# Query and key projections of the second attention as seven half-size products per 1024 columns

## The chip, the core and the metric
The kernel runs on one core of one Trainium2 chip. The core has five engines with queues of their own: TensorE (PE; PEld is its weight load), VectorE (DVE), ScalarE (ACT), GpSimd (POOL), and SyncE (SP), which here only issues transfers. Each engine takes its instructions in order and waits on semaphores for the others. The metric is device microseconds of one execution, lower is better.

## What is computed
Two transformer-like blocks run one after the other on a sequence of 1024 tokens of width 1024, all in fp32. Of the second block this matters:

```python
h = rms_norm(x, norm1_g)
proj = jnp.einsum('bsd,de->bse', h, w_in)          # 1024 x 1024 by 1024 x 6144
q, k, v, bg, cg, xc = jnp.split(proj, [1024, 2048, 3072, 4096, 5120], axis=-1)
# 16 heads of 64 columns: q and k are normalised per head, then chunked attention
q = rms_norm(q.reshape(..., 16, 64), q_norm_g)
k = rms_norm(k.reshape(..., 16, 64), k_norm_g)
```

The columns of q, k and v are wanted token-major (tokens on the partitions). The other columns (bg, cg, xc) and the gates are computed feature-major inside the attention phase, as filler work for TensorE.

## The kernel before
**Arithmetic.** Each fp32 operand is split into a high part, rounded to the matmul type fp32r, and a low part, the rest. A product is three matmul passes: high by high, high by low, low by high (`three_passes`, L199). A matmul multiplies a 128x128 block of one side by 128x512 of the other into one of the 8 banks of `ps`. The high part of the activations lies in `a_hi`, the low part in `a_lo`, each 128 partitions x 8 blocks of 128 features x 1024 tokens.

**Weights.** SP loads a chunk of 1 MB into `w_raw`; GpSimd makes `w_hi` and `w_lo` of it (`pieces`, L156: four adds of zero, then four subtractions). There are two slots of each. A chunk of the "wide" kind is 512 input features x 512 columns.

**Order of the phases around the change.** `phase_norm` (L1478) does the first block's output projection, adds the residual, normalises with the next block's gain, turns the rows (transposes into `ps`), splits them into `a_hi` (ScalarE) and `a_lo` (VectorE, function `low`), and then already computes the first 512 value columns (`next_half`). `phase_tm` (L520) computes the other five groups of 512 columns: q and k (four groups, per-head normalised by VectorE after the product) and, last, the second half of v (not normalised). `phase_attention` (L1787) loads head by head from the DRAM tensor `qkv2`. At the start of it TensorE computes four products of the feature-major filler (`EARLY = 4`, 24 matmuls each, numbered x = 0 to 3); after x = 1 and x = 2 it turns the first head's queries and keys (`round_`), and then the scores begin. `phase_turn` (L211) stands at the start of each phase: every engine but TensorE waits there until the other three have arrived, which closes the buffers of the old phase.

One group of 512 columns in `phase_tm` is 8 token tiles x 8 feature blocks x 3 passes = 192 matmuls. It is done in two halves (first 512 features for all 8 tiles, then the other 512). VectorE copies each finished bank to `stage_tm`, squares, reduces, scales; ScalarE takes the root and issues the 2 MB store of the group.

**Engine load in the MLP, for comparison.** The last phase, `phase_mlp` (L2553), already multiplies by Strassen's scheme. Its instructions there serve as rows for the new ones here: ScalarE's `w_hi` (L2892), GpSimd's `w_lo` (L2795), VectorE's `a_lo` (L3019), its additions of a bank to `res` (L3099) and its sums of two quarters (L3014).

Of the kernel before, what the change touches and what calls it, by code (L numbers as in the profile page):

```python
# [13 lines left out]
P = 128  # L14
T = 1024
# [29 lines left out]
class Tally:  # L45


    def __init__(self, sem):
        self.sem, self.base = sem, 0
# [5 lines left out]
def program(nc, io, out):  # L55
    ctx = ExitStack()
    with ctx:
# [17 lines left out]
        ext2 = dram("ext2", (16, P, 768))  # L75
        row1 = dram("bias_row1", (8, 512))
# [26 lines left out]
        W_V2 = seg(io["w_in_2"], 0, 2048, 2, wide=2)  # L103
        W_QK2 = seg(io["w_in_2"], 0, 0, 8, wide=2)
        seg(io["w_in_2"], 0, 2560, 2, wide=2)
# [378 lines left out]
        mm_tm = sem("mm_tm")  # L484
        ev_tm = sem("ev_tm")
        st_tm = [sem(f"st_tm{s}") for s in range(2)]
        tm_chunks = [2]
        tm_stores = [0, 0]
# [17 lines left out]

        def wide_first(pe, n, slot, c):

            pe.wait_ge(split_done, n + 1)
            for t in range(NT):  # L510
                pe.wait_ge(ev_tm, c * 8 + (2 * t - 6))
                wide_unit(t, t, slot, 0).then_inc(mm_tm, 1)

        def wide_second(pe, n, slot):

            pe.wait_ge(split_done, n + 1)
            for t in range(NT):
                wide_unit(t, t, slot, 1).then_inc(mm_tm, 1)

        def phase_tm(start, sections, dst, stored):  # L520

            per, width = 2, 512
            groups = sum(n for n, _, _ in sections)
            count = groups * per
            c0 = tm_chunks[0]
            tm_chunks[0] += count
            v0 = list(tm_stores)
            tm_stores[0] += (groups + 1) // 2  # L530
            tm_stores[1] += groups // 2
            heads = width // HD
            with ExitStack() as mem:
                phase_turn()
                stage = sb(mem, f"stage_tm{start}", [P, 2, NT, width])
                if any(normed for _, _, normed in sections):
                    square = sb(mem, "head_square", [P, NT * heads, HD])
                    hst = sb(mem, "head_stat", [P, 6, NT * heads])
                    h_sq, h_root, h_self, h_done = sem("h_sq"), sem("h_root"), sem("h_self"), sem("h_done")
                feed(block, start, count, lambda j: (mm_tm, j * 8 + (c0 * 8 + 8)))  # L540
                dst_v = dst.rearrange("(t p) n -> p t n", p=P)
                unstored = []

                def each_chunk(eng, body):

                    j0 = 0
                    for n, col0, normed in sections:
                        if n > 1:
                            with eng.Fori(0, n // 2) as i:
                                for q in range(2):  # L550
                                    body(i * 2 + (j0 + q), q, i + j0 // 2, i * (2 * width) + (col0 + q * width), normed)
                        if n % 2:
                            body(j0 + n - 1, 0, (j0 + n) // 2, col0 + (n - 1) * width, normed)
                        j0 += n

                @block.tensor
                def _(pe):
                    def chunk(j, q, before, col, normed):
                        wide_first(pe, j * 2 + start, slot_of(start), j * 2 + c0)
                        wide_second(pe, j * 2 + (start + 1), slot_of(start + 1))  # L560
                    each_chunk(pe, chunk)
# [60 lines left out]
        def phase_first():  # L622
# [611 lines left out]
            for r in row_in:  # L1234
                r.base += 32
# [1974 lines left out]
```

## Time and profile before
| what | value |
|---|---|
| median of 3 runs | 2184.09 us (2184.08 to 2185.55) |
| span of the profiled execution | 2181.7 us |
| median less that span | 2.4 us |
| PE busy, share of the span | 99% |
| DVE, ACT, POOL busy | 64%, 40%, 46% |
| granted TensorE clock, mean | 0.999 |

The profile shows one execution, from its first to its last instruction. What lies around the span (2.4 us) belongs to the launch. The median of the runs is what a time of the kernel means below. "Busy" of TensorE counts an instruction until its modelled end; since matmuls overlap, the spacing of their starts is what shows the pace.

### The profile page before, as it was taken

What the parts mean: (1) busy time and instruction counts of PE and PEld (TensorE: products, weight loads), DVE (VectorE), ACT (ScalarE), POOL (GpSimd) and SP (SyncE); (2) the same over time, 40 slices, a digit from 0 to 9 for tenths busy, and PEclk for the clock granted to TensorE, in tenths of its full rate; (3) what the DMA queues carried; (4) which work ended last, traced back from release to release, by engine and by line L of the source; (5) the groups of instructions that cost most, each with busy time, mean ns of one, the idle gap of its engine ahead of it and who ended that gap; (6) DMA issues with size and microseconds to landing.
All of it is one profiled execution on the core that took longest, in us unless ns stands there. A gap on an engine that the chain in (4) does not pass through costs nothing.

```text
span 2181.7 us, 29189 instructions
## 1 busy us (share of the span) xinstructions
PE 2165.9 (99%) x10570; PEld 1810.3 (83%) x10570; DVE 1406.0 (64%) x2453; ACT 862.3 (40%) x1584; POOL 994.3 (46%) x715
## 2 busy tenths in 40 slices
PE   8999999999999999999999999999999999999999
PEld 8888888888888888888888888888878888788887
DVE  7776775234445666666666493342786777898886
ACT  5555424200005555555555231212555455433332
POOL 3233465554443231313222274447465655666564
PEclk9999999999999999999999999999999999999999
DMA  6320123213225332324232473215134545826433
GB/s 230 104 75 21 45 102 140 107 43 131 96 90 154 93 93 87 106 69 112 75 99 69 167 256 118 99 62 183 59 125 157 172 145 183 327 90 229 149 123 115
DMA packets 195688, 267.17 MB, mean 122 GB/s; under 512 B 57912, under 2 KB 114008, under 8 KB 195584
## 3 DMA queue, kind: packets, MB, share of 16 engines
q1 hardware_dynamic: 119456, 189.85, 25.4%
q10 hardware_dynamic: 76128, 75.93, 11.1%
q8 instruction: 66, 1.08, 0.2%
q14 instruction: 38, 0.31, 0.0%
HBM read 190.19 MB, written 83.95 MB: 126 GB/s over the span
## 4 chain that ended last, share of the span: by engine, by line
PE 92%; DVE 3%; ACT 2%; issue 1%; POOL 1%; DMA 0%; ACTq 0%; DVEq 0%; POOLq 0%
PE ps L204 80%; PE ps L1916 3%; PE ps L1903 2%; PE ps L1891 2%; PE ps L891 1%; PE ps L866 1%; PE ps L877 1%; DVE k_lo L2137 1%; POOL w_lo L2775 1%; PE ps L1928 1%; DVE pt_lo L2185 0%; ACT pt_hi L2071 0%; PE ps L801 0%; DVE prob L2166 0%; PE ps L2410 0%
## 5 line engine op out<-in xcount | busy, mean ns | idle before, releaser
L159 POOL TENSOR_TENSOR w_hi<-w_raw,zero 128x512 fp32r<-128x512 f32 x216 | 260.3, 1236 | 865.1 <-PE ps L204 756.5
L204 PE MATMUL ps<-a_hi,w_hi 128*128 128x512 f32 x1408 | 542.9, 406 | 0.4 <-DVE q_st L1138 0.4
L204 PE MATMUL ps<-a_hi,w_lo 128*128 128x512 f32 x1408 | 523.3, 392 | 0.0
L204 PE MATMUL ps<-a_lo,w_hi 128*128 128x512 f32 x1408 | 520.6, 390 | 0.0
L204 PE MATMUL ps<-w_hi,a_hi 128*128 128x512 f32 (+1 forms) x1088 | 419.0, 385 | 3.7 <-POOL w_lo L787 2.2
L204 PE MATMUL ps<-w_hi,a_lo 128*128 128x512 f32 (+1 forms) x1088 | 417.4, 384 | 0.0
L204 PE MATMUL ps<-w_lo,a_hi 128*128 128x512 f32 (+1 forms) x1088 | 417.1, 383 | 0.0
L204 PEld LDWEIGHTS ps<-a_hi,w_lo 128*128 128x128 f32 x1408 | 264.2, 188 | 58.7
L204 PEld LDWEIGHTS ps<-a_lo,w_hi 128*128 128x128 f32 x1408 | 265.4, 189 | 41.9
L204 PEld LDWEIGHTS ps<-a_hi,w_hi 128*128 128x128 f32 x1408 | 264.8, 188 | 42.5 <-issue 0.8
L164 POOL TENSOR_TENSOR w_lo<-w_raw,w_hi 128x512 fp32r<-128x512 f32 x216 | 293.9, 1392 | 4.2
L204 PEld LDWEIGHTS ps<-w_hi,a_hi 128*128 128x128 f32 x1088 | 204.9, 188 | 45.8 <-POOL w_lo L787 2.4
L204 PEld LDWEIGHTS ps<-w_hi,a_lo 128*128 128x128 f32 x1088 | 205.0, 188 | 40.3
L204 PEld LDWEIGHTS ps<-w_lo,a_hi 128*128 128x128 f32 x1088 | 205.1, 188 | 39.9
L2185 DVE TENSOR_TENSOR pt_lo<-ps,pt_hi 128x512 fp32r<-128x512 f32 (+1 forms) x192 | 88.2, 487 | 146.7 <-ACT pt_hi L2071 146.7
L2055 ACT ACTIVATE prob<-prob,st 128x640 f32<-128x640 f32 (+4 forms) x128 | 89.4, 698 | 223.4 <-DVE st L2166 222.4
L2775 POOL TENSOR_TENSOR w_lo<-mlp_raw_b,w_hi 128x512 fp32r<-128x512 f32 x60 | 97.5, 1651 | 63.0 <-ACT w_hi L2861 63.0
L571 DVE COPY stage_tm<-ps 128x512 f32<-128x512 f32 x40 | 27.7, 691 | 149.9 <-PE ps L204 149.9
L2795 POOL TENSOR_TENSOR w_lo<-mlp_raw_more,w_hi 128x512 fp32r<-128x512 f32 x56 | 90.1, 1639 | 61.1 <-ACT w_hi L2892 61.1
L3019 DVE TENSOR_TENSOR a_lo<-mlp_part,a_hi 128x512 fp32r<-128x512 f32 x104 | 108.4, 1090 | 4.8 <-ACT a_hi L2901 4.8
L2166 DVE CUSTOM_DVE_ANT_0 prob<-ps,bias 128x640 f32<-128x640 f32 (+4 forms) x128 | 83.6, 653 | 23.5 <-issue 22.8
L2775 POOL TENSOR_TENSOR w_lo<-w_raw,w_hi 128x512 fp32r<-128x512 f32 x44 | 69.8, 1612 | 51.2 <-ACT w_hi L2861 51.2
(270 smaller groups left out, 3481.6 us busy)
## 6 DMA issues: line engine op xcount, KB each, us to landing
w_raw<-in_w_in_dram SPq DMA_DIRECT2D x32, 1024.0 KB, 5.1
mlp_part<-u_parts SPq DMA_DIRECT2D x26, 1024.0 KB, 7.8
feat_fm<-stage ACTq DMA_DIRECT2D x68, 256.0 KB, 2.0
u_parts<-mlp_acc SPq DMA_DIRECT2D x28, 512.0 KB, 2.8
u_parts<-res SPq DMA_DIRECT2D x28, 512.0 KB, 2.8
conv_in<-feat_fm ACTq DMA_DIRECT2D x24, 512.0 KB, 5.6
qkv_tm<-stage_tm ACTq DMA_DIRECT2D x5, 2048.0 KB, 6.9
res<-in_x_dram SPq DMA_DIRECT2D x16, 512.0 KB, 6.3
```

The source lines that it names most:

```text
L159: hi = nc.gpsimd.tensor_tensor(w_hi[slot][:, k:k + 2, :], w_raw[:, k:k + 2, :], zero[:, 0:1].unsqueeze(2).to_broadcast([P, 2, CW]), ALU.add)
L164: lo = nc.gpsimd.tensor_tensor(w_lo[slot][:, k:k + 2, :], w_raw[:, k:k + 2, :], w_hi[slot][:, k:k + 2, :].bitcast(F32), ALU.subtract)
L204: last = nc.tensor.matmul(out_of(o), lhs, rhs(o), start=first and n == 0, stop=final and n == 2)
L1891: last = nc.tensor.matmul(ps[:, S_BANK + bank, 0:c1 - c0], q_st[:, head_slot, b * P:(b + 1) * P], kk[:, head_slot, k0 * P + c0:k0 * P + c1 ...
L1903: last = nc.tensor.transpose(ps[:, PT_BANK + j // 4, (j % 4) * P:(j % 4 + 1) * P], prob[:, m % 4, j * P:(j + 1) * P], ident[:, :])
L1916: last = nc.tensor.matmul(ps[:, O_BANK, 0:256], v_st[:, h, kb, :], pt[:, sl, :], start=(kb == first and pt is pt_hi), stop=(kb == last_kb ...
L2055: nc.scalar.activation(prob[:, s, 0:w], prob[:, s, 0:w], ACT.Exp, scale=-1.0, bias=st[:, s, 1:2], accum_out=st[:, s, 2:3]).then_inc(exped, 1)
L2166: nc.vector.tensor_tensor_reduce(out=tile_view(prob, s, 0, nk), in0=score_view(nk), in1=tile_view(bias, hh, off, nk), scale=-1.0, scalar=3 ...
L2185: ins = nc.vector.tensor_tensor(pt_lo[:, sl:sl + cnt, cols], ps[:, bank, 0:cnt * P].rearrange("p (j n) -> p j n", n=P), pt_hi[:, sl:sl + c ...
L2775: ins = nc.gpsimd.tensor_tensor(low[:, k:k + 2, :], up_raw(p)[:, k:k + 2, :], high[:, k:k + 2, :].bitcast(F32), ALU.subtract)
L2795: ins = nc.gpsimd.tensor_tensor(down_slot(w_lo, s)[:, k, :], raw_of[p][h][:, k, :], down_slot(w_hi, s)[:, k, :].bitcast(F32), ALU.subtract)
L3019: nc.vector.tensor_tensor(down_operand(a_lo, s)[:, k, :], staged(s)[:, k, :], down_operand(a_hi, s)[:, k, :].bitcast(F32), ALU.subtract).t ...
```

## The change
Queries and keys are now computed, 1024 columns at a time (a "unit": unit 0 is q, unit 1 is k), by one step of Strassen's scheme. Tokens, features and columns are each cut in two. Seven products of 512 tokens x 512 features x 512 columns take the place of eight. The seven are called m1 to m7 and run in the order m5, m2, m4, m3, m1, m7, m6, numbered s = 0 to 13 over both units. Five of the seven need a sum of two weight quarters, five need a sum of two activation quarters. The results are added into the four quarters of the output, which lies in `res`. Each product has 4 token tiles x 4 feature blocks x 3 passes = 48 matmuls.

What moves with it:
- The second half of the value columns comes first, and ScalarE evicts and stores it. Queries and keys come last before the attention.
- ScalarE makes the weights' high part (two instructions of 128x1024 per product), GpSimd only the low part (four of 128x512). The high part of product s + 2 waits until product s has left its slot.
- VectorE sums weights, adds banks into `res`, and does the head norm per quarter (four quarters per unit). ScalarE does the squares and evicts the first two products of a unit.
- In `phase_norm` VectorE also writes an fp32 copy of the turned rows into `res` (eight copies of 128x1024 out of `ps`), which the sums need. Half of it is stored to DRAM (`spare_x`) and loaded back at the end, because two quarters of `a_hi` and `a_lo` are overwritten and the attention's filler needs them plain again (`plain_hi`, `plain_lo`).
- `ready_first` for the first head of the attention now names the stores of the quarters that hold its columns; the last store of a 2 MB value group in the attention phase goes.

The core of the diff:

```diff
-            last_store = phase_tm(W_QK2, [(4, 0, True), (1, 2560, False)], qkv2, stored2)
+            banks_read, ready_first, ready_rest = phase_qkv(stored2, spare_stored)
@@ phase_norm, vector
                     def low(t):
                         dve.wait_ge(n_hi.sem, hi0 + t + 1)
+                        if post:
+                            dve.wait_ge(*x1_stored[t % 4].at(16 * (t // 4 + 1)))
+                            nc.vector.tensor_copy(res[:, t, :].rearrange("p (k n) -> p k n", n=P), both(t))
                         nc.vector.tensor_tensor(a_lo[:, :, t * P:(t + 1) * P], both(t), ...)
@@ phase_norm, scalar
+                    def store_spare(t):
+                        act.wait_ge(n_lo.sem, lo0 + t + 1)
+                        act.dma_start(spare_x[t // 4, :, :, t % 4 * P:(t % 4 + 1) * P], turned_row(t, 0 if t // 4 else 4)
+                                      ).then_inc(spare_stored.sem, 16)
@@ new: phase_qkv
+            ORDER = ("m5", "m2", "m4", "m3", "m1", "m7", "m6")
+            COPIED = {"m5": ((0, 0, -1.0), (1, 0, 1.0)), "m2": ((0, 1, 1.0), (1, 1, -1.0))}
+            ADDED = {"m4": ((0, 0), (0, 1)), "m3": ((1, 0), (1, 1)), "m1": ((0, 0), (1, 1)), "m7": ((0, 0),), "m6": ((1, 1),)}
+            WHOLE = {"m4": (0, 1), "m3": (1, 0), "m7": (0, 0), "m6": (1, 1)}
+            SUMMED = ("m5", "m2", "m1", "m7", "m6")
+                def _(pool):
+                    for s in range(NS):
+                        for half in range(2):
+                            pool.wait_ge(*high_w.at(2 * s + half + 1))
+                            for k in (2 * half, 2 * half + 1):
+                                ins = nc.gpsimd.tensor_tensor(wide(w_lo, s)[:, k, :], raw_of[ORDER[s % 7]][:, k, :],
+                                                              wide(w_hi, s)[:, k, :].bitcast(F32), ALU.subtract)
+                        ins.then_inc(low_w.sem, 1)
+                def _(pe):
+                    for s in range(NS):
+                        p = ORDER[s % 7]
+                        pe.wait_ge(*low_w.at(s + 1))
+                        for t in range(4):
+                            (waits until copied or added of product s - 2, tile t)
+                            for k in range(4):
+                                last = three_passes(...)
+                            last.then_inc(mm_q.sem, 1)
+                    pe.wait_ge(plain_lo, 2)
+                def _(act):
+                    for s in range(NS):
+                        p = ORDER[s % 7]
+                        if p in COPIED:
+                            if s >= 7:
+                                for r, c, _ in COPIED[p]:
+                                    act.wait_ge(*store_q[r, c].at(16))
+                            for t in range(3):
+                                copy_tile(s, t)
+                        if s + 2 < NS:
+                            weight_high(s + 2)   # waits: product s done, weight sum of s + 2 done
+                        if p in COPIED:
+                            copy_tile(s, 3)
+                        if p in WHOLE:
+                            squares(s)           # one ACTIVATE of 128x2048, then the root
+                        if s == NS - 2:
+                            for n, q in enumerate(("m4", "m3")):
+                                act.wait_ge(*spare_in.at(16 * (n + 1)))
+                                nc.scalar.activation(operand(q)[0], (rd, rb)[n], ACT.Copy).then_inc(plain_hi, 1)
+                def _(dve):
+                    for s in range(NS):
+                        p = ORDER[s % 7]
+                        if p in ADDED:
+                            for t in range(4):
+                                add_tile(s, t)   # one 128x512 addition per quarter named in ADDED
+                        ahead = {1: 3, 2: 3, 3: 3, 5: 2, 6: 2}.get(s % 7)
+                        if ahead is not None and s + ahead < NS:
+                            weight_sum(s + ahead)   # two of 128x1024
+                        if p in WHOLE:
+                            norm_heads(s)        # reduce, six small ones, four products of 128x512
+                        if s == NS - 2:
+                            for n, q in enumerate(("m4", "m3")):
+                                dve.wait_ge(plain_hi, n + 1)
+                                nc.vector.tensor_tensor(operand(q)[1], (rd, rb)[n], ...).then_inc(plain_lo, 1)
```

## Rows read from the trace of the kernel before

**Rows 1.** The page: busy time and share of each engine
```profile
PE 2165.9 (99%) x10570; PEld 1810.3 (83%) x10570; DVE 1406.0 (64%) x2453; ACT 862.3 (40%) x1584; POOL 994.3 (46%) x715
```

**Rows 2.** Chain that ended last, 330 to 700 us: start us, us, what
```profile
398.15 0.87 PE ps L1578 x8
399.02 261.15 PE ps L204 x1152
660.18 0.44 PE ps L1928 x4
...
671.99 0.17 PE ps L1891 x2
```

**Rows 3.** Busy time of each engine over the whole of `phase_tm`
```profile
434.00:650.00 216.00, 216.00 (x954) 178.92 (x953) 95.99 (x76) 1.39 (x4) 106.66 (x80) 1.00 0.25 88
```

**Rows 4.** DVE and POOL in order of time, 474 to 494 us, head norm
```profile
476.05 4.57 DVE L576 TENSOR_TENSOR head_square<-stage_tm 128x4096 f32<-128x4096 f32 x1
480.65 4.42 DVE L577 TENSOR_REDUCE head_stat<-head_square 128x64 f32<-128x4096 f32 x1
485.49 0.55 DVE L580 RECIPROCAL head_stat<-head_stat 128x64 f32<-128x64 f32 x1 [0.41 <-ACT head_stat L597]
486.31 1.19 DVE L582 TENSOR_TENSOR head_stat<-head_stat 128x64 f32<-128x64 f32 x1
489.01 0.23 DVE L585 TENSOR_TENSOR head_stat<-head_stat 128x64 f32<-128x64 f32 x1
489.27 4.43 DVE L587 TENSOR_TENSOR stage_tm<-stage_tm,head_stat 128x4096 f32<-128x4096 f32 x1
...
475.30 8.22 POOL L159 TENSOR_TENSOR w_hi<-w_raw,zero 128x512 fp32r<-128x512 f32 x4 [12.62 <-PE ps L204]
483.59 5.07 POOL L164 TENSOR_TENSOR w_lo<-w_raw,w_hi 128x512 fp32r<-128x512 f32 x4
```

**Rows 5.** DVE, POOL and ACT in order of time, 2047.9 to 2060.5 us, MLP
```profile
2047.96 1.28 DVE L3099 TENSOR_TENSOR res<-res,ps 128x512 f32<-128x512 f32 x2 [0.36 <-PE ps L204]
2050.52 6.51 DVE L3019 TENSOR_TENSOR a_lo<-mlp_part,a_hi 128x512 fp32r<-128x512 f32 x4 [1.27 <-ACT a_hi L2901]
2056.95 1.21 DVE L3014 TENSOR_TENSOR mlp_acc<-mlp_acc 128x1024 f32<-128x1024 f32 x1
...
2050.04 6.44 POOL L2795 TENSOR_TENSOR w_lo<-mlp_raw_more,w_hi 128x512 fp32r<-128x512 f32 x4 [4.87 <-ACT w_hi L2892]
...
2047.96 2.01 ACT L2892 ACTIVATE w_hi<-mlp_raw_more 128x1024 fp32r<-128x1024 f32 x2 [6.79 <-PE ps L204]
```

**Rows 6.** DVE and ACT in order of time, 387 to 403 us, end of `phase_norm`
```profile
389.61 0.15 DVE L1735 TENSOR_SCALAR stat_n<-stat_n 128x1 f32<-128x1 f32 x1 [1.02 <-ACT stat_n L1643]
...
391.78 1.21 DVE L1750 TENSOR_TENSOR a_lo<-ps,a_hi 128x1024 fp32r<-128x1024 f32 x1
...
393.84 1.99 DVE L1745 SCALAR_TENSOR_TENSOR mt_n<-res,stat_n,gpre_n 128x1024 f32<-128x1024 f32 x1
396.49 1.23 DVE L1750 TENSOR_TENSOR a_lo<-ps,a_hi 128x1024 fp32r<-128x1024 f32 x1 [0.66 <-ACT a_hi L1672]
...
395.44 1.03 ACT L1672 ACTIVATE a_hi<-ps 128x1024 fp32r<-128x1024 f32 x1 [2.78 <-PE ps L1578]
```

**Rows 7.** ACT and its queue in order of time, 649 to 663 us
```profile
650.57 1.15 ACTq L1991 DMA_DIRECT2D qk_raw<-qkv_tm  x2
...
656.23 0.63 ACT L2012 ACTIVATE v_st<-v_raw 128x512 fp32r<-128x512 f32 x1 [40.22 <-DMA qk_raw<-qkv_tm]
656.77 0.58 ACT L2019 ACTIVATE stage<-ps 128x512 f32<-128x512 f32 x1
```

**Rows 8.** DMA issues: KB each, median us from issue to landing
```profile
w_raw<-in_w_in_dram SPq DMA_DIRECT2D x32, 1024.0 KB, 5.1
...
u_parts<-res SPq DMA_DIRECT2D x28, 512.0 KB, 2.8
```

**Rows 9.** TensorE, 10.2 to 22.4 us: busy, granted clock
```profile
10.20:14.00 3.80, 1.58 (x12) 1.00 1.04 408
14.00:15.60 1.60, 1.53 (x9) 0.71 1.03 412
15.60:19.00 3.40, 3.40 (x21) 0.63 1.03 375
19.00:22.40 3.40, 3.40 (x30) 1.00 0.67 208
```

More of the change, by code:

```diff
@@ L481, in phase_merge @@
             return opened, (ev_fm, u0 + 20)
-        mm_tm = sem("mm_tm")
         ev_tm = sem("ev_tm")
-        st_tm = [sem(f"st_tm{s}") for s in range(2)]
-        tm_chunks = [2]
-        tm_stores = [0, 0]
+        again = {}
         def tm_unit(t, bank, col, slot, b_hi, b_lo, ks):
@@ L1235, in phase_first, with reused @@
                 r.base += 32
+            for n, s_ in enumerate(raw_part):
+                again[f"raw_part{n}"] = (s_, 16)
+            for n, s_ in enumerate(bias_in):
+                again[f"bias_in{n}"] = (s_, 64)
+            again.update(tab_in=(tab_in, 48), gain_in=(gain_in, 16), sink_in=(sink_in, 16), normed=(normed, NT + 1),
+                         turned_x=(turned_x, NT + 1), x_hi=(x_hi, NT + 1), x_lo=(x_lo, NT + 1), kv_mm=(kv_mm, NT),
+                         kf_in=(kf_in, NT), kt=(kt, NT), v_hi=(v_hi, NT), v_lo=(v_lo, NT), qhi=(qhi, 8), qlo=(qlo, 8),
+                         khi=(khi, 2), klo=(klo, 2), scored=(scored, STEPS), maxed=(maxed, STEPS), exped=(exped, STEPS),
+                         scaled=(scaled, STEPS), turned=(turned, STEPS), pthi=(pthi, STEPS), ptlo=(ptlo, STEPS),
+                         valued=(valued, STEPS // 2), o_half=(o_half, STEPS // 2), o_done=(o_done, STEPS // 2))
+        def reused(name):
+            return Tally(*again.pop(name))
         def phase_mix():
@@ L1665, in x_stats @@
                         act.wait_ge(*n_added.at(t + 1))
[L1666 removed]
+                        act.dma_start(x_dst[t * P:(t + 1) * P, :], res[:, t, :]).then_inc(x1_stored[t % 4].sem, 16)
                         square(res[:, t, :], stat[:, t, 8:9])
@@ L1691, in _ @@
                             x_stats(s - 1)
+                        if post and s >= lag + 1:
+                            store_spare(s - lag - 1)
+                    if post:
+                        store_spare(NT - 1)
                     if post:
@@ L1781, in phase_norm @@
             for tally, n in ((n_hi, NT), (n_lo, NT), (n_mm_l, 2 * NT), (n_out_l, NT), (n_mm_r, NT), (n_prepared, NT),
-                             (n_added, NT), (n_normed, NT), (n_turned, NT), *((r, 32) for r in row_in), (n_stored, 16 * 2 * NT if post else 0)):
+                             (n_added, NT), (n_normed, NT), (n_turned, NT), *((r, 32) for r in row_in), (n_stored, 16 * NT if post else 0)):
                 tally.base += n
-            return n_stored.at(0)
-        def phase_attention(pairs, src, q_col, k_col, v_col, back, ext, norm_gains, w_start, dst, last_store, banks_read, ready_first, ready_rest):
+            return n_stored.at(0), spare_stored.at(16 * NT)
@@ L1795, in phase_attention @@
+        def phase_attention(pairs, src, q_col, k_col, v_col, back, ext, norm_gains, w_start, dst, banks_read, ready_first, ready_rest):
             nslot = back + 2
```

368 lines of the change are left out of this document (262 added, 106 removed).

## The prediction, made blind
> **What bounds the kernel now.** I read the page first: TensorE is busy 99% of the span, the others 64%, 40% and 46% [rows 1]. Then the chain that ended last, around the phases in question: one unbroken piece of 1152 matmuls in 261.15 us, from the last transposes of `phase_norm` to the first turn of a head [rows 2]. It holds 144 matmuls of the value columns in `phase_norm`, five groups of 192 in `phase_tm`, and 48 of the attention's first two filler products: 144 + 960 + 48 = 1152. So TensorE alone sets the time here, at 261.15 / 1152 = 0.2267 us a matmul. The third view, busy time over `phase_tm`, shows how much the others have to spare: of 216 us VectorE works 96.0, ScalarE 1.4, GpSimd 106.7 [rows 3]. Fewer matmuls shorten the kernel by their full time, as long as the others can feed the new scheme at its pace. That is the question.
>
> **What goes.** Four groups of 192 matmuls become 14 products of 48: 768 - 672 = 96 fewer. 96 x 0.2267 = 21.8 us less. A product lasts 48 x 0.2267 = 10.88 us, and this is each engine's budget per product. The value group is only moved.
>
> **The prices.** An addition of a bank into `res`: two in 1.28 us, so about 0.61 each when queued. A sum of 128x1024 on VectorE 1.15, two of them (one weight sum) 2.3. ScalarE makes a chunk's high part in 2.01, its first half in 1.0 [rows 5]. GpSimd's low part takes 5.05 for four pieces when VectorE leaves it alone [rows 4]. In the new code GpSimd starts behind ScalarE's first half, so weights are ready 1.0 + 5.05 + 0.25 for hops = 6.3 us after a late weight sum. The head norm of a quarter (128x2048): the reduction half of 4.42, 2.2; the root with its hops 0.5; six small ones 1.5 (they took 3.8 on twice the width, of which about 2 were spent waiting for GpSimd); the scaling half of 4.43, 2.3 with gaps. Sum 6.6 [rows 4]. ScalarE's square of 128x2048: 1.03 for 1024 [rows 6], 0.58 for 512 [rows 7], hence some 1.9.
>
> **VectorE and GpSimd hold each other up.** GpSimd's four adds of zero last 8.22 us over a VectorE instruction of 4.57, that is 3.65 without it; VectorE's `L582` takes 1.19 where its like `L585` takes 0.23 [rows 4]. In the MLP four `a_lo` and four `w_lo` side by side take 6.5 each, against 0.6 and 1.26 a piece alone [rows 4, 5]. So a VectorE instruction with both inputs in SBUF waits up to 1.0 us for a piece of GpSimd's, and the reverse. Reductions and bank additions don't. Weight sums, scalings and small products of the new phase do.
>
> **Is VectorE fast enough?** Per unit it has 28 bank additions (17.1), four of its five sums (9.2) within the dense stretch, and four norms (26.4): 53 us of 76, and what comes to it is bunched. I follow it from the end of product m4 of unit 0 (s = 2), where its first dense stretch starts; times in us from there. Last two additions 1.2; sum for m7 with one wait 3.3; norm 6.8: 11.3 (product 3 ended at 10.9). Additions of m3 4.9: 16.2. Sum for m6 2.7: 18.9. Norm, beside GpSimd's pieces, 6.8 + 3.6 of waits: 29.3. Additions of m1 and m7 7.3: 36.6. Sum for the next m5 2.4: 39.0; weights at 45.3. TensorE has finished product 6 at 4 x 10.88 = 43.5. **Stall before product 7: 1.8.** Then ScalarE first does the weights' high part and only then the square for m7's quarter, 4.0: 43.0; norm 6.8: 49.8; additions of m6 2.4; sum for m2 2.4: 54.6; weights at 60.9. Product 7 ended at 45.3 + 10.9 = 56.2. **Stall before product 8: 4.7.** Together 6.5. The bounds: without any of the 5 us of mutual waits, product 7 comes in time and only 2.9 remain before product 8; with waits of 1.1 in place of 1.0 and 0.68 for an addition, the mean of all of these in the MLP's long stretches, the stalls grow to about 10.
>
> **The end of the phase.** Before, the value group stood between the keys and the attention; now nothing does. I count from the end of product 9 (m4 of unit 1). Same steps as above: 11.3, 16.2, sum 3.2 (19.4), norm 10.3 (29.7), additions of m1 and m7 7.3 (37.0). Now no sum; the square has to be waited for, 2.0 (39.0); norm 6.7 (45.7); then the two `plain_lo` of 128x2048, 2.3 each by the same row as the scaling (50.3); then the first two additions of product 13, which free the bank of the first filler product, 1.3: 51.6. TensorE ended product 13 at 43.5. **Stall before the filler: 8.1.** The spare rows are not late: they are loaded in products 10 to 12, each some 5 us [rows 8]. GpSimd's split of the first filler chunk begins at product 12's end and takes 9.1: hidden.
>
> Further: two more additions 1.2 (52.8), square 2.0, norm 6.7 (61.5), `phase_turn` 0.6 (62.1). Only here can head 0 be loaded, since `phase_turn` waits for VectorE's last norm, though its own quarters were stored long before. In the profile of before the loads went out at 650.57 and the value split that waits for all of them began at 656.23: 5.7 [rows 7]. The 1 MB store of the last quarter (2 x 2.8 [rows 8]) runs beside them; between 0 and 4 us for it, I take 1.7. Landed: 69.5. TensorE's two filler products end at 51.6 + 10.9 = 62.5. **Stall before the first turn: 7.0.** Behind it product x = 2 needs its bank read, which stands behind the value split in ScalarE's queue: 0.63 + 0.58 less the turn's 0.44 [rows 2, 7], **0.9** with the hop. Before, the head had landed 4 us ahead of its turn [rows 2, 7].
>
> **`phase_norm`.** VectorE's eight copies out of `ps` cost some 1.2 each. In each round VectorE stands idle for 1.0 us until ScalarE's root [rows 6], which takes most of a copy. At the end the `a_lo` that at 396.49 ended 1.3 us before TensorE wanted it at 399.02 [rows 2, 6]; with two copies ahead of it (one delays the normalisation at 393.84, its own is the other) it ends at about 399.5. **0.5.** Bounds 0 and 2. ScalarE's spare stores cost its queue 0.35 each and wait for nothing late.
>
> **TensorE's clock.** Early in the kernel TensorE worked 1.58 of 3.8 us, and the granted clock in the 5 us behind that was 0.71 and 0.63, then full again [rows 9]; at full clock that stretch of 3.4 us holds 30 matmul records, at the lower 21. The nearest row therefore says that a stall of 4 us or more costs a further 3.4 us at half speed, 1.6 us of work. Three stalls here are as long. What is lost in the first filler product is taken out of the wait that follows it; two remain: **3.2**, bounds 0 and 5. By the Trainium skill ("TensorE: Matmul & The Clock Gate", section Why this matters for your kernels) idle gaps between bursts of matmuls send TensorE back to the half clock. The trace agrees at its only such place, with 0.63; a sum that leaves the clock alone would be 3.2 lower. Restarting behind a wait costs about 0.2 (weight load, first matmul), four times: **0.8**.
>
> **The sum.** 1.8 + 4.7 + 8.1 + 7.0 + 0.9 + 0.5 + 3.2 + 0.8 = 27.0 lost, 21.8 gained: **5.2 slower**. The profiled execution would have a span of 2181.7 + 5.2 = 2186.9; the median lies 2.4 above the span, so **2189.3**. About 0.2%, 4.4 us, is what a measurement of this kernel can tell from no change.
>
> **Rivals.**
> 1. *The balance.* The same stalls, but smaller by a few us (the clock doesn't fall, or the store doesn't delay the head, or half of the mutual waits are missing). Then loss and gain cancel within 4.4 us: 2180 to 2188. For it: most of the waits are counted by chance meetings. Chance 0.30.
> 2. *VectorE keeps up.* Its mutual waits with GpSimd are the mechanism: without them the first stretch ends with a stall of 2.9, the second with 4.1 before the filler (product 12's end + 0.6 + 2.0 + 6.7 + 4.6 + 1.3 against 10.9), and the head comes 5.0 late. 2.9 + 4.1 + 5.0 + 0.9 + 0.5 + 0.8, with one fall of the clock 1.6: 15.8 lost, 6.0 gained, 2178. It decides from about 9 us less loss than in my sum. Against it: both pairs of rows that show the waits. Chance 0.14.
> 3. *The chain slips further.* In unit 0 VectorE frees the bank of m1's tile only 1.4 us before product 6 wants it, so with the MLP's slower means product 6 is late too, and both ends grow: 10 + 10.6 + 8.5 + 0.9 + 2 + 5 + 0.8 = 37.8, 16 slower, 2200. Chance 0.04.
> 4. My forecast, 4.4 to 13 us slower: 0.52.
>
> **Range.** Rivals 1 and 2 are of the other signs, so the range reaches into them: 2179 to 2197; the likeliest case alone 2188.5 to 2197. Faster 0.14, same 0.30, slower 0.56.
>
> **What would show it.** Right: 96 fewer matmuls; in `phase_qkv` TensorE gaps before products 7 and 8 released by GpSimd's `w_lo`, one before the filler released by VectorE (`plain_lo` or the addition), one before the first turn released by a transfer of `qk_raw`; VectorE nearly without idle time from product 2 to product 6 and from 9 to the end; a granted clock below 1.0 behind the long gaps. Wrong: VectorE idle before the additions of m1; the gap before product 7 absent; a head that lands before the second filler product ends; or a gap at the first products, if the activation sums (20 of 128x512) and their first 12 low parts came later than the value group's 43.5 us hide. I count those at 20 x 0.65 + 12 x 0.65 and up to 9 of waits beside GpSimd's split, 30 us, covered.

## The result, and the profile after

The changed kernel takes 2192.07 us, median of 5 runs (2191.75 to 2194.76), against 2184.26 us for the kernel before, run beside it (5 runs, 2184.08 to 2185.55). The ratio is 1.0037, 95% interval 1.0025 to 1.0049: slower by 7.8 us. The prediction was 2189.3, 5.2 slower, range 2179 to 2197.

The page of the changed kernel, span and busy time of each engine, answers to [rows 1]:

```profile
span 2190.5 us, 29152 instructions
PE 2155.1 (98%) x10474; PEld 1797.8 (82%) x10474; DVE 1481.8 (68%) x2599; ACT 941.6 (43%) x1686; POOL 983.5 (45%) x707
```

The matmuls are 96 fewer, 10570 - 10474, as the change says. TensorE is busy 10.8 us less than in [rows 1], but the span is 8.8 us longer. So TensorE now waits, and part of its work runs slower.

Where it waits is seen in the chain that ended last, the view of [rows 2]. Before it was one piece of 1152 matmuls; now it passes to VectorE for most of the phase:

```profile
400.10 109.12 PE ps L203 x480
509.24 1.28 DVE res L1985 x2
510.52 3.39 DVE qkv_raw L1974 x2
513.91 2.21 DVE qkv_head_stat L1992
...
534.27 5.22 DVE res L2003 x3
...
549.03 2.01 ACT w_hi L1886 x2
551.04 1.82 ACT qkv_spare L1897
...
561.94 2.28 DVE qkv_raw L1974 x2
564.31 1.07 ACT w_hi L1886
565.44 5.03 POOL w_lo L1830 x4
570.52 23.67 PE ps L203 x96
...
642.53 2.29 DVE a_lo L2034
644.82 2.40 DVE res L1985 x4
...
657.34 7.63 DMA qk_raw<-qkv_tm
665.01 1.11 PE ps L2182 x4
```

`L203` is the matmul, `L1974` a weight sum, `L1985` a bank addition, `L1992` and `L2003` the reduction and scaling of the head norm, `L1886` and `L1830` the weights' high and low parts, `L1897` ScalarE's square, `L2034` a plain low part, `L2182` the first turn. From 509.24, the end of product 2, the chain is additions, sums and norms until ScalarE and GpSimd hand over the weights of product 8 at 570.52. The longest piece of another engine before that is 3.8 us: from 549.03 ScalarE first makes product 7's high part and then the square for the quarter of m7, and VectorE waits for that square. After products 8 and 9 it is VectorE's again, until the additions that free the filler's bank and the load of head 0.

TensorE in order of time shows the four waits, in brackets with what released them: product 7, product 8, the filler, the first turn.

```profile
555.31 0.50 PE L203 MATMUL ps<-w_hi,a_hi 128*128 128x512 f32 x1 [1.63 <-POOL w_lo L1830]
...
570.52 0.53 PE L203 MATMUL ps<-w_hi,a_hi 128*128 128x512 f32 x1 [4.03 <-POOL w_lo L1830]
...
646.16 0.76 PE L203 MATMUL ps<-a_hi,w_hi 128*128 128x512 f32 x1 [7.51 <-DVE res L1985]
...
665.01 1.11 PE L2182 MATMUL ps<-ident,qk_raw 128*128 128x128 f32 x4 [6.23 <-DMA qk_raw<-qkv_tm]
```

Busy time of each engine from the value group to the first turn, the view of [rows 3]:

```profile
core 0: us, PE busy (x) PEld busy (x) DVE busy (x) ACT busy (x) POOL busy (x), PEclk, DMA share, GB/s
435.00:665.00 230.00, 210.60 (x904) 171.45 (x902) 163.89 (x220) 81.14 (x107) 108.82 (x80) 0.97 0.32 105
```

VectorE had 96.0 of 216 us of work; it now has 163.9 of 230, and TensorE's mean clock in the stretch is 0.97.

VectorE, then GpSimd, 510 to 540 us: a scaling and four low parts of weights, each once alone and once beside the other, and a reduction beside low parts.

```profile
513.83 2.27 DVE L1992 TENSOR_REDUCE qkv_head_stat<-qkv_spare 128x32 f32<-128x2048 f32 x1
...
518.57 2.50 DVE L2003 TENSOR_TENSOR res<-res,qkv_head_stat 128x512 f32<-128x512 f32 x4
...
532.66 6.82 DVE L2003 TENSOR_TENSOR res<-res,qkv_head_stat 128x512 f32<-128x512 f32 x4
...
510.54 7.07 POOL L1830 TENSOR_TENSOR w_lo<-qkv_raw,w_hi 128x512 fp32r<-128x512 f32 x4 [5.75 <-ACT w_hi L1886]
521.26 5.10 POOL L1830 TENSOR_TENSOR w_lo<-qkv_raw,w_hi 128x512 fp32r<-128x512 f32 x4 [3.65 <-ACT w_hi L1886]
532.46 6.48 POOL L1830 TENSOR_TENSOR w_lo<-qkv_raw,w_hi 128x512 fp32r<-128x512 f32 x4 [6.10 <-ACT w_hi L1886]
```

The scaling takes 2.50 alone and 6.82 beside GpSimd's pieces, which themselves take 6.48 in place of 5.10. The reduction runs beside GpSimd's pieces (510.54 to 517.61) and takes 2.27, as long as the next one, at 528.50, with GpSimd idle.

**The account, by the trace.** I add up TensorE's start-to-start times beyond 0.2267 us a matmul, from the value group to the first scores:

| term | forecast | measured |
|---|---|---|
| before product 7 | 1.8 | 1.8 |
| before product 8 | 4.7 | 4.2 |
| before the filler | 8.1 | 7.7 |
| before the first turn with the bank behind it; a lower clock in the filler product counted in, as in the forecast | 7.9 | 7.2 + 1.6 = 8.8 |
| restarts | 0.8 | 0.1 behind product 7, the others in the terms beside them |
| `phase_norm` | 0.5 | 0.4 |
| clock behind product 8's wait and behind the first turn | 3.2 | 1.7 + 1.8 = 3.5 |
| pace of products m1, m7, m6 | none | 1.9 |
| constants' load landed later, before anything that the change touches | none | 0.9 |
| **lost** | **27.0** | **29.3** |
| 96 matmuls | -21.8 | -21.8 |

29.3 - 21.8 = 7.5, and the first scores come at 679.4 in place of 671.8. In the rest of the span, 1511 us, another 1.3 us is lost.

This is the account of one execution. In a second one of the same kernel (`e8_changed_again` below; span 2190.2) nothing starts late, the wait before the turn is 5.8, and the falls of the clock cost 2.8 behind product 8's wait, 2.0 in the filler and 2.2 behind the turn, where the first has 1.7, 1.6 and 1.8. The first three waits are stable, the size of a fall is not.

### The profile page after: what moved, and what is told of

It reads as the page before. It is cut to its first block, busy times and chain, and to the rows that moved or that the text cites. A ratio compares the mean times of both kernels' runs of the same rounds, so it can differ in the third digit from the quotient of the medians.

```text
span 2190.5 us, 29152 instructions
## 1 busy us (share of the span) xinstructions
PE 2155.1 (98%) x10474; PEld 1797.8 (82%) x10474; DVE 1481.8 (68%) x2599; ACT 941.6 (43%) x1686; POOL 983.5 (45%) x707
## 4 chain that ended last, share of the span: by engine, by line
PE 82%; DVE 8%; ACT 3%; issue 3%; POOL 2%; DMA 1%; ACTq 0%; DVEq 0%; SPq 0%; POOLq 0%
PE ps L203 71%; PE ps L2170 3%; PE ps L2157 2%; PE ps L2145 2%; DVE res L1985 1%; PE ps L778 1%; DVE res L2003 1%; DVE qkv_raw L1974 1%; PE ps L753 1%; PE ps L764 1%; DVE qkv_head_stat L1992 1%; DVE k_lo L2390 1%; POOL w_lo L3028 1%; PE ps L2182 1%; DVE pt_lo L2438 0%
## 5 line engine op out<-in xcount | busy, mean ns | idle before, releaser
L158 POOL TENSOR_TENSOR w_hi<-w_raw,zero 128x512 fp32r<-128x512 f32 x184 | 209.3, 1168 | 785.3 <-PE ps L203 662.1
L203 PE MATMUL ps<-a_hi,w_hi 128*128 128x512 f32 x1408 | 544.8, 407 | 8.3 <-DVE res L1985 7.5
L203 PE MATMUL ps<-a_hi,w_lo 128*128 128x512 f32 x1408 | 524.6, 393 | 0.0
L203 PE MATMUL ps<-a_lo,w_hi 128*128 128x512 f32 x1408 | 522.3, 391 | 0.0
L203 PE MATMUL ps<-w_hi,a_hi 128*128 128x512 f32 (+1 forms) x960 | 370.1, 386 | 9.7 <-POOL w_lo L1830 5.7
L203 PE MATMUL ps<-w_hi,a_lo 128*128 128x512 f32 (+1 forms) x960 | 368.4, 384 | 0.0
L203 PE MATMUL ps<-w_lo,a_hi 128*128 128x512 f32 (+1 forms) x960 | 368.0, 383 | 0.0
L203 PEld LDWEIGHTS ps<-a_hi,w_lo 128*128 128x128 f32 x1408 | 265.0, 188 | 58.8
L203 PEld LDWEIGHTS ps<-a_hi,w_hi 128*128 128x128 f32 x1408 | 265.8, 189 | 51.6 <-issue 9.6
L203 PEld LDWEIGHTS ps<-a_lo,w_hi 128*128 128x128 f32 x1408 | 266.4, 189 | 42.0
L163 POOL TENSOR_TENSOR w_lo<-w_raw,w_hi 128x512 fp32r<-128x512 f32 x184 | 255.5, 1420 | 3.6
L203 PEld LDWEIGHTS ps<-w_hi,a_hi 128*128 128x128 f32 x960 | 181.2, 189 | 48.1 <-POOL w_lo L1830 6.5
L203 PEld LDWEIGHTS ps<-w_hi,a_lo 128*128 128x128 f32 x960 | 181.1, 189 | 35.7
L203 PEld LDWEIGHTS ps<-w_lo,a_hi 128*128 128x128 f32 x960 | 181.1, 189 | 34.9
L1830 POOL TENSOR_TENSOR w_lo<-qkv_raw,w_hi 128x512 fp32r<-128x512 f32 x48 | 70.0, 1490 | 90.2 <-ACT w_hi L1886 90.2
L3028 POOL TENSOR_TENSOR w_lo<-w_raw,w_hi 128x512 fp32r<-128x512 f32 x44 | 69.1, 1598 | 53.2 <-ACT w_hi L3114 53.2
```

The lines of the kernel that those rows point to most:

```text
L158: hi = nc.gpsimd.tensor_tensor(w_hi[slot][:, k:k + 2, :], w_raw[:, k:k + 2, :], zero[:, 0:1].unsqueeze(2).to_broadcast([P, 2, CW]), ALU.add)
L163: lo = nc.gpsimd.tensor_tensor(w_lo[slot][:, k:k + 2, :], w_raw[:, k:k + 2, :], w_hi[slot][:, k:k + 2, :].bitcast(F32), ALU.subtract)
L203: last = nc.tensor.matmul(out_of(o), lhs, rhs(o), start=first and n == 0, stop=final and n == 2)
L1830: ins = nc.gpsimd.tensor_tensor(wide(w_lo, s)[:, k, :], raw_of[ORDER[s % 7]][:, k, :], wide(w_hi, s)[:, k, :].bitcast(F32), ALU.subtract)
L3028: ins = nc.gpsimd.tensor_tensor(low[:, k:k + 2, :], up_raw(p)[:, k:k + 2, :], high[:, k:k + 2, :].bitcast(F32), ALU.subtract)
```

## The experiments

All are edits of the changed kernel. Ratios are to the kernel before, timed beside each of them: 2184.82 us for the first three, 2184.29 for the next four, 2184.32 for the three after that, 2184.25 for the last. Differences to the changed kernel are taken from 2192.07, above, for the first three and from 2192.20, the changed kernel again, for the others.

### Without the head norm

The kernel leaves out the square and the norm of the heads in `phase_qkv`, so its queries and keys are not normalised; the stores wait for the last additions in place of the norm.

```diff
-                        if p in WHOLE:
-                            squares(s)
...
-                        if p in WHOLE:
-                            norm_heads(s)
```

> Leaves out the head norm of queries and keys (ScalarE's squares and roots, VectorE's reductions and scalings); each quarter is stored once its last product is added. Theory (VectorE's queue sets the four stalls): with 26.4 us less on VectorE per unit all four stalls close, and what 96 fewer matmuls are worth stands alone: the time before, 2184.3, less 21.8, plus 0.4 in phase_norm and at most 2 at the first turn: 2163 to 2165. Rival (loads of weight quarters, GpSimd's low parts or ScalarE's order set the stalls): gaps before products 7 and 8 stay at some 2 and 4 us and the time is above 2170.

2170.32 us (2170.02 to 2172.82), ratio 0.9936, 0.9919 to 0.9952: 21.8 less than the changed kernel. Its waits, TensorE in order of time:

```profile
632.39 0.50 PE L203 MATMUL ps<-a_hi,w_hi 128*128 128x512 f32 x1 [2.20 <-POOL w_lo L163]
...
644.93 0.66 PE L2179 MATMUL ps<-ident,qk_raw 128*128 128x128 f32 x4 [1.33 <-DMA qk_raw<-qkv_tm]
646.08 0.50 PE L203 MATMUL ps<-a_hi,w_hi 128*128 128x512 f32 x1 [0.49 <-ACT stage L2270]
```

The waits before products 7 and 8 are gone, and so are the falls of the clock. So the head norms set these stalls. The edit takes VectorE's part of them and ScalarE's squares away at once, so it doesn't divide the stalls between the two. It came out 5 to 7 us above the expectation, and its 2170.3 is as high as the rival account asked for; what speaks against that account is that the waits it kept are gone. `L163`, GpSimd's split of the filler chunk, now meets VectorE's plain low parts and is late by 2.2; the head still comes 1.3 late and its bank 0.5; and 1.9 us is the slower pace that no theory had. These are 5.9 of the 7.

### One weight sum drawn forward

The sum for m2 of unit 1 (product 8) is made right behind the one for product 7, in place of behind product 6's additions and the norm.

```diff
-                        ahead = {1: 3, 2: 3, 3: 3, 5: 2, 6: 2}.get(s % 7)
+                        ahead = {1: 3, 2: 3, 3: 3, 5: 2}.get(s % 7)
...
+                            if s == 5:
+                                weight_sum(8)
```

> VectorE makes the weight sum of unit 1's m2 right behind that of its m5 (at s = 5), no longer behind the norm of m7's quarter and the additions of m6. Theory: product 8's weights are then ready before product 7 ends, its gap of 4.2 us and the half clock behind it (1.7) go, product 7 stays 1.8 late: 2192.1 - 5.9 = 2186.2. Rival (the load of that weight quarter or GpSimd holds product 8): the gap stays, 2192.

2188.56 us (2187.70 to 2190.09), 1.0017, 1.0007 to 1.0026. The wait before product 8 is gone, but that before product 7 grew:

```profile
555.27 0.79 PE L203 MATMUL ps<-w_hi,a_hi 128*128 128x512 f32 x1 [2.51 <-POOL w_lo L1830]
```

The sum now runs beside the pieces of product 7's own low part, which wait for it (5.95 us in place of 5.09 in the changed kernel); and the clock fell behind this longer wait (0.51 in the 3.5 us after it). 3.5 us were won, not 5.9. What stands in the way of the rest is the next consumer, product 9, whose weights GpSimd finishes at 578.96:

```profile
573.88 5.08 POOL L1830 TENSOR_TENSOR w_lo<-qkv_raw,w_hi 128x512 fp32r<-128x512 f32 x4 [12.73 <-ACT w_hi L1886]
```

```profile
579.02 0.50 PE L203 MATMUL ps<-w_hi,a_hi 128*128 128x512 f32 x1
```

TensorE begins it at 579.02. By my estimate, with product 7 at 554.4 as in the changed kernel and no fall, it would have come there at 554.4 + 96 x 0.2267 = 576.2 and waited. The high part behind these weights stands in ScalarE's queue behind the square for m6's quarter, which waited 8.8 us for VectorE's additions. The order of VectorE's queue sets which product waits.

### Plain low parts and product 13's additions ahead of the last two norms

ScalarE likewise makes the plain high parts before the square.

```diff
                         if p in ADDED:
                             for t in range(4):
                                 add_tile(s, t)
...
-                        if p in WHOLE:
+                        if p in WHOLE and s < NS - 2:
                             norm_heads(s)
...
+                    norm_heads(NS - 2)
+                    norm_heads(NS - 1)
```

> VectorE and ScalarE restore the plain operands and add product 13 before the last two head norms. Theory (the filler's stall and the head's stall lie on two branches of the same VectorE queue; only the head's landing sets the time): the gap before the filler shrinks from 7.7 to about 1, the one before the first turn grows from 6.4 to about 9 to 11, and the sum falls only by what VectorE no longer idles, 3 to 5 us: 2187 to 2189. Rival (the gaps are separate costs): the filler's 7.7 come back in full, 2184.4.

2189.78 us (2187.49 to 2191.42), 1.0020, 1.0011 to 1.0030, 0.8 above the expected stretch: a small miss.

```profile
641.25 0.50 PE L203 MATMUL ps<-a_hi,w_hi 128*128 128x512 f32 x1 [2.27 <-POOL w_lo L163]
...
662.23 1.12 PE L2184 MATMUL ps<-ident,qk_raw 128*128 128x128 f32 x4 [9.80 <-DMA qk_raw<-qkv_tm]
```

The filler's wait fell by 5.2 and the turn's grew by 3.6. Both waits hang on one queue, VectorE's: what goes first there only chooses which of them is long.

### Head 0's queries and keys loaded early

The tiles for head 0's queries and keys are opened before `phase_qkv`, and SP issues their loads there once the two quarters are stored, without waiting for `phase_turn`. The head's gains are loaded early too, and its values are split one step later. A form that also loads the values early (`e3_head_early`) needs more SBUF than the phase leaves, and has no time.

```diff
                         if not more:
+                            sp.wait_ge(*store_q[0, 0].at(32))
+                            sp.wait_ge(*store_q[1, 0].at(32))
+                            src_v = qkv2.rearrange("(t p) n -> p t n", p=P)
+                            sp.dma_start(qk_raw[:, :, 0, :], src_v[:, :, 0:HD]).then_inc(head_in, 16)
+                            sp.dma_start(qk_raw[:, :, 1, :], src_v[:, :, 1024:1024 + HD]).then_inc(head_in, 16)
                             load_weights(sp, W_BCX2 + 1, W_BCX2 + 2)
```

> SP loads the first head's queries and keys (buffers of their own) and the norm gains before the phase ends, as soon as the quarters that hold them are stored; the head's values are loaded behind the phase change as before and are split one step later. Theory: the gap of 6.4 us before the first turn goes, with the half clock behind it (1.7), the 7.7 before the filler stay: 8.1 below the changed kernel, 2184. Rival (the first head waits for ScalarE and VectorE to enter the attention phase as much as for its data): the gap moves behind the turn and less than 4 us are won.

2183.98 us (2182.80 to 2185.71), 0.9999, 0.9990 to 1.0009: 8.2 below the changed kernel timed beside it. The filler's own wait stays; what remains behind the filler is a wait for a bank:

```profile
645.31 0.77 PE L203 MATMUL ps<-a_hi,w_hi 128*128 128x512 f32 x1 [7.36 <-DVE res L1992]
...
658.57 0.50 PE L203 MATMUL ps<-a_hi,w_hi 128*128 128x512 f32 x1 [0.32 <-ACT stage L2278]
```

6.2 - 0.3 us of waiting, and the 1.8 of the clock behind it, make 7.7. This is the largest gain of one edit here that keeps the norm, and the loss was `phase_turn`'s, not the arithmetic's.

### Tiles of the sums moved by 64 bytes

```diff
+                sb(mem, "qkv_pad", [P, 16])
                 op_h = sb(mem, "qkv_op_hi", [P, 3, 4, 512], F32R)
```

> A pad of 64 bytes a partition is put ahead of the tiles that hold the summed activations; nothing else. In the changed kernel every second matmul of m1, m7 and m6 starts 0.240 us after the one before it, all others 0.2267. Theory (where the tile lies sets the pace): the 0.240 goes and 6 x 24 x 0.0133 = 1.9 us with it, 2190.2. Rival (other engines' work beside these products): the pace stays.

2191.95 us (2190.69 to 2194.02), 1.0033, 1.0021 to 1.0046, 0.25 below the changed kernel: no measurable difference. Summed over products m1, m7, m6 the excess over 0.2267 a matmul goes from 0.9 + 0.9 to 0.8 + 0.8 us. Moving them by 64 bytes is worth 0.0009 us a matmul; the cause of the pace stays open.

### TensorE kept at work in the waits, and the changed kernel again

34 transposes of the identity, whose result nothing reads, run while TensorE waits for product 8's weights, and 50 behind the filler.

```diff
+                        if s == 8:
+                            pe.wait_ge(*added.at(added_to(6, 0)))
+                            for _ in range(34):
+                                nc.tensor.transpose(ps[:, 0, 0:P], ident[:, :], ident[:, :])
...
+                        if x == 1:
+                            for _ in range(50):
+                                nc.tensor.transpose(ps[:, 0, 0:P], ident[:, :], ident[:, :])
```

> TensorE does 34 idle transposes while it waits for product 8 and 50 while it waits for the first turn; they end before the waits do. Theory (the clock's fall behind a long gap costs time of its own): the granted clock stays at 1.0 behind both, 1.7 and 1.6 us less, 2188.8. Rival (what is lost at half clock is covered by the next wait): no change, 2192.

> The changed kernel itself, as the base on this chip: 7.8 us above the kernel before; gaps of 1.8, 4.2, 7.7 and 6.4 us.

With transposes 2187.70 us (2187.10 to 2190.34), 1.0016, 1.0007 to 1.0026; without, 2192.20 (2191.53 to 2193.97), 1.0038, 1.0023 to 1.0052. TensorE's windows behind product 8's wait: busy with the count of matmuls, granted clock. First the changed kernel:

```profile
569.50:573.00 3.50, 3.37 (x8) 0.50 0.03 5
573.00:576.50 3.50, 3.50 (x12) 0.68 0.48 181
576.50:580.00 3.50, 3.50 (x17) 1.00 0.32 119
```

and with the transposes:

```profile
569.50:573.00 3.50, 3.31 (x15) 1.00 0.00 0
573.00:576.50 3.50, 3.50 (x17) 1.00 0.46 172
```

Product 8 begins at the same time in both (569.69 with transposes). 0.50 is the lower of the clock's two levels, 1.2 GHz. Work without use, put where TensorE would have stood still, is worth 4.5 us here: two falls of the clock. By the starts the two falls cost 2.8 + 2.2 in the kernel without transposes.

### The two that helped, together

The weight sum drawn forward and head 0 early.

> The early sum of m2 and the early load of the first head's queries and keys together. Theory (the two stretches of the phase are separate, what each saves adds up): product 7 some 2.5 late with a fall of the clock, product 8 in time, the filler 7.7 late, the first turn in time: 3.6 + 8.2 below the changed kernel, 2180.4, that is 3.9 below the kernel before. Rival (the second stretch takes back what the first gives): 2184.

2181.03 us (2180.21 to 2182.56), 0.9985, 0.9975 to 0.9994. What is left is a wait of 2.24 before product 7 and 7.36 before the filler.

### Plain low parts on GpSimd

In addition GpSimd makes the two plain low parts, and ScalarE the filler chunk's high part, which GpSimd made itself by adding zero. ScalarE makes these high parts ahead of the square for m7's quarter.

```diff
+                    for n, q in enumerate(("m4", "m3")):
+                        pool.wait_ge(plain_hi, n + 1)
+                        for k in range(4):
+                            ins = nc.gpsimd.tensor_tensor(operand(q)[1][:, k, :], (rd, rb)[n][:, k, :],
+                                                          operand(q)[0][:, k, :].bitcast(F32), ALU.subtract)
+                        ins.then_inc(plain_lo, 1)
...
-                        if s == NS - 2:
-                            for n, q in enumerate(("m4", "m3")):
-                                dve.wait_ge(plain_hi, n + 1)
-                                nc.vector.tensor_tensor(operand(q)[1], (rd, rb)[n], operand(q)[0].bitcast(F32),
-                                                        ALU.subtract).then_inc(plain_lo, 1)
```

> As e9, and GpSimd makes the plain low parts (it idles between the last product's weights and the filler's), while ScalarE makes the high part of the filler's first chunk. Theory (VectorE's two plain low parts, 5.6 us, and its place in the queue behind the norm of m7's quarter set the filler's start; the head's landing does not): the filler is 1 to 2.5 late in place of 7.7, no fall of the clock there, the turn in time or up to 1 late: 2184.3 - 21.8 + 0.4 (phase_norm) + 2.5 + 2.4 (clock behind product 7's gap) + 2 + 0.5 + 1.9 (pace of m1, m6, m7) + 1 = 2173.2. Rival (GpSimd itself becomes late with ten us more of work, or the head lands too late for an earlier filler): the loss moves to GpSimd's split or the turn, 2178 or more.

2178.40 us (2177.58 to 2180.23), 0.9973, 0.9963 to 0.9982: faster than the kernel before by 5.9 and than the changed one by 13.8. The expectation was too low by 5: the filler still waits 5.4, and product 9, which no expectation had, 1.65.

```profile
578.82 0.50 PE L203 MATMUL ps<-w_hi,a_hi 128*128 128x512 f32 x1 [1.65 <-POOL w_lo L1837]
...
640.00 0.76 PE L203 MATMUL ps<-a_hi,w_hi 128*128 128x512 f32 x1 [5.38 <-DVE res L2010]
```

VectorE in order of time says why: the additions of product 13 stand behind the norm of m7's quarter, and that norm behind ScalarE's square, with VectorE idle for 1.98.

```profile
621.43 7.25 DVE L2010 TENSOR_TENSOR res<-res,ps 128x512 f32<-128x512 f32 x12
630.66 2.29 DVE L2017 TENSOR_REDUCE qkv_head_stat<-qkv_spare 128x32 f32<-128x2048 f32 x1 [1.98 <-ACT qkv_spare L1917]
...
638.57 2.48 DVE L2010 TENSOR_TENSOR res<-res,ps 128x512 f32<-128x512 f32 x4
```

### The same with 18 transposes before product 7

```diff
+                        if s == 7:
+                            pe.wait_ge(*added.at(added_to(5, 0)))
+                            for _ in range(18):
+                                nc.tensor.transpose(ps[:, 4, 0:P], ident[:, :], ident[:, :])
```

> As e10, with 18 idle transposes on TensorE while it waits for product 7. Theory (a gap of 2.5 us cost 2.4 more at half clock): the clock stays at 1.0, 2.4 less than e10. Rival (the fall there is covered by later waits): the same as e10.

2178.66 us (2177.93 to 2180.41), 0.9973, 0.9962 to 0.9983: no gain, a miss. The window behind this wait explains it in part. In the kernel with the two edits together the clock had fallen there; in the one with the plain parts on GpSimd, behind a wait of the same 2.24 us, it had not. First the former, then the latter:

```profile
555.20:558.70 3.50, 3.50 (x9) 0.54 0.00 0
```

```profile
555.20:558.70 3.50, 3.50 (x16) 1.00 0.00 0
```

But the fall had cost the former nothing either. Its TensorE begins product 9 at the same time as the latter's (578.82, with a wait of 1.65, in the lines above):

```profile
578.78 0.50 PE L203 MATMUL ps<-w_hi,a_hi 128*128 128x512 f32 x1
```

In both, product 9's weights are ready only then. So the rival account held: what is lost at half clock before a product that is late anyway is covered by that product's wait.

### Two tiles of product 13 ahead of the norm

This and its expectation start from the kernel with the plain parts on GpSimd (2178.4).

```diff
-                            for t in range(4):
+                            for t in range(2 if s == NS - 1 else 0, 4):
                                 add_tile(s, t)
+                        if s == NS - 2:
+                            for t in range(2):
+                                add_tile(NS - 1, t)
```

> The sixth-but-last kernel of this series (value sum drawn forward, head 0's queries and keys early, GpSimd making the plain low parts), with one more move: VectorE adds the first two tiles of product 13 before it norms the quarter of m7, not after it. In that kernel TensorE waited 5.38 us before the filler, released by an addition of product 13 that stood behind this norm on VectorE, while GpSimd's split of the filler chunk was done near 635.3. By my account (the wait is a matter of VectorE's queue) the two additions fit into the time in which VectorE waits for ScalarE's square, the gap falls from 5.4 to about 0.7, and up to half of that comes back as a later last norm, so a wait of some us before the first turn: 2 to 4 us below 2178.4, about 2175.5. By the rival account (the last norm sets the end anyway, and the filler's wait is only moved to the turn) the time stays at 2178, with the gap before the turn grown by what the gap before the filler lost.

2179.47 us (2178.37 to 2180.17), 0.9977, 0.9968 to 0.9986: no gain. TensorE's waits:

```profile
635.84 0.50 PE L203 MATMUL ps<-a_hi,w_hi 128*128 128x512 f32 x1 [0.62 <-POOL w_lo L1853]
...
650.24 1.09 PE L2205 MATMUL ps<-ident,qk_raw 128*128 128x128 f32 x4 [3.21 <-DVEq L2392]
652.45 0.80 PE L203 MATMUL ps<-a_hi,w_hi 128*128 128x512 f32 x1 [1.12 <-ACT stage L2296]
```

The filler starts 4.2 us earlier, and 3.2 + 1.1 come back before and behind the turn (with the granted clock at 0.50 from 650.3 to 653.8), released by the memories that open once VectorE's last norm is done (`DVEq` is VectorE's sequencer at the attention's first wait). The rival account held: the last norm sets the end.

## Why the prediction was right

**The main step held: fewer matmuls, and VectorE's queue takes more back.** The counted gain of 21.8 is exact. The four waits stand where they were put, with the releasers that were named, and the first three are within 0.5 us. VectorE has no idle time worth naming from product 2's end to the sum for product 7, and that sum ends 39.9 us behind it, forecast 39.0. The kernel without the head norm shows that the norms, with their squares on ScalarE, are what costs: its waits before products 7 and 8 are gone. Two counts of the prediction are off without touching its sum: a unit has 32 bank additions, not 28, and in rival 2 the terms before the filler give 4.3, not 4.1.

**The mutual waits of VectorE and GpSimd held**, and with them the ground against rival 2: 2.50 to 6.82 for one scaling, 5.10 to 6.48 for the pieces. The reduction at 513.83, beside the pieces, keeps its 2.27. The Trainium skill (SBUF — State Buffer, section SBUF: two separate sides) says that a VectorE instruction with two SBUF inputs and a GpSimd instruction that reads SBUF exclude one another for their whole length; the trace agrees with those numbers. The kernel with one sum drawn forward shows it once more: product 7's pieces, now beside a sum, took 5.95 in place of 5.09, and its wait grew from 1.6 to 2.5.

**The head's load held** as a cause: the turn waits for `qk_raw`, and the early load took 8.2 us off. With the filler's lower clock counted in, as the forecast did, the wait was 0.9 larger than forecast, 8.8 for 7.9: the chain has 7.6 for the transfers, where 5.7 + 1.7 was counted, and the filler's wait came out 0.4 shorter, which lengthens this one by as much. The 1.7 for the store beside the loads was picked between 0 and 4; no run separates it.

**The clock held in kind; its size is part luck.** It fell behind product 8's wait, in the filler and behind the turn (granted clock 0.69, 0.55 and 0.50 in the 3.5 us from 569.5, 646.2 and 666.0), each 1.6 to 1.8 us, forecast 1.6. In the second execution of the same kernel the three cost 2.8, 2.0 and 2.2. By the rule of the Trainium skill weighed in the prediction ("TensorE: Matmul & The Clock Gate", section Why this matters for your kernels) such gaps send TensorE back to the half clock; the trace agrees at these three places. The pair of kernels with and without transposes measures two of the falls at 4.5 us by the medians, between the 3.5 and the 5.0 that the starts give in the two executions.

**What failed: the sum had no term for the pace.** "96 x 0.2267" took every remaining matmul at 0.2267. In products m1, m7 and m6 the mean is 0.2333, 6 x 48 matmuls, 288 x 0.0067 = 1.9 us. That, 0.9 us by which this profiled run started late, and the 0.9 at the turn make most of the difference between 27.0 and 29.3; product 8, the filler and the restarts come out 1.7 lower. The late start is no part of the change: it is there before any changed instruction, and the other kernels of this series lie between. In the second execution it is absent, and larger falls of the clock fill its place (29.8 lost in all); no run shows a link between the two.

**Rivals.** Rival 1, the balance, had its conditions unmet in the changed kernel. The kernel with the head loaded early, which is not one of its conditions but takes away what the store could delay, came to that balance: 0.9999. Rival 3 didn't come: product 6 isn't late.

**Open.** The cause of the slower pace; the kernel without the norm has it too, so VectorE's norms beside it are not the cause. And the 1.3 us lost behind the first scores: 0.7 of it lies in the attention, where every changed kernel has 0.5 to 2.0 more than the kernel before from first to last scores, though its instructions are the same. I made no experiment on either beyond the 64 bytes.

## What to carry to other kernels

A cut in matmuls is worth its time only as far as the engines that prepare operands keep up product by product: lay out each one's queue against the product's length, with the collisions of VectorE and GpSimd in it, before counting the gain. When a wait is caused by a queue, reordering it moves the wait to the next consumer; taking work off the queue, or cutting the dependence (the loads behind `phase_turn`), shortens or removes it. Once TensorE has waits of some us, the clock's fall behind each costs up to 2.8 us more in these executions (1.1 the least), and work without use inside the wait can give it back, but only where the next product isn't late by itself.

## What the runs showed of the hardware

**Two paces at one clock.** Matmuls of one form, 128x512 at granted clock 1.00, start 0.2267 us apart on average when the activations lie in `a_hi` and `a_lo`, and 0.2333 when they lie in `qkv_op_hi` and `qkv_op_lo`. It is not that the activations are sums: those of m5 and m2 are too, but lie in `a_hi` and `a_lo`, and have the faster pace. With the pad the mean is 0.2324, and 0.2343 in the kernel with the head loaded early and those built on it. TensorE in order of time, product 4 of the changed kernel; the starts are 0.230 and 0.237 apart in turn (the pad's expectation says 0.2267 and 0.240):

```profile
520.62 0.39 PE L203 MATMUL ps<-w_hi,qkv_op_hi 128*128 128x512 f32 x1
520.85 0.40 PE L203 MATMUL ps<-w_lo,qkv_op_hi 128*128 128x512 f32 x1
521.09 0.39 PE L203 MATMUL ps<-w_hi,qkv_op_lo 128*128 128x512 f32 x1
521.32 0.40 PE L203 MATMUL ps<-w_hi,qkv_op_hi 128*128 128x512 f32 x1
```

**The clock behind waits of nearly the same length.** Behind 1.4 to 1.6 us before product 7 it stayed in every kernel; behind 2.51 it fell (one kernel); behind 2.24 it fell in two kernels and stayed in one; behind 2.20 and 2.27 before the filler it stayed; behind 3.21 before the turn it fell. A gain that rests on a wait of 2 to 2.5 us is not to be counted on either way.
